# Chunk decays of a state-space layer: from a mask addition on VectorE to products with scaled lower triangles

## The reference

```
acum  = cumsum(dt * A)                       # over the 128 tokens of a chunk
decay[i, j] = exp(acum[i] - acum[j]) for j <= i, else 0
wgt   = (C . B)[i, j] * decay[i, j] * dt[j]
y     = wgt @ x  +  exp(acum) * (C @ h_start)
h_end = exp(acum[last]) * h_start + sum_j exp(acum[last] - acum[j]) dt[j] x[j] B[j]
```

## Time and profile before

| | |
|---|---|
| time before, median of 3 runs | 2368.07 us (2365.31 to 2373.49) |
| profiled execution, its time | 2380.31 us |
| its span | 2378.5 us |
| busy: TensorE products, weight loads | 1704.0 us (72%), 1171.4 us (49%) |
| busy: VectorE, ScalarE, GpSimd | 1596.6 us (67%), 492.7 us (21%), 930.1 us (39%) |
| granted TensorE clock, mean of the span | 0.817 of 2.4 GHz |

### The profile page before, as it was taken

One profiled execution on the slowest core, in us unless ns is written; L12 is line 12 of the kernel. 1 busy time (PEld: TensorE's weight loads), 2 busy tenths in 40 slices (PEclk: granted clock), 3 DMA queues, 4 the chain that ended last, 5 costly groups with the idle time before them and its releaser, 6 DMA issues.

```text
span 2378.5 us, 30817 instructions
## 1 busy us (share of the span) xinstructions
PE 1704.0 (72%) x10511; PEld 1171.4 (49%) x10511; DVE 1596.6 (67%) x4212; ACT 492.7 (21%) x1458; POOL 930.1 (39%) x840
## 2 busy tenths in 40 slices
PE   7999976687897898966999979993544444344434
PEld 7899966443686776754678757670100000000000
DVE  5634178877668537988566775637288878877854
ACT  3335233200144123222123320110011000010000
POOL 0000001145433443533554554657644444444441
PEclk9999988757899999988999989997655655555656
DMA  6487757279999999966999999989999999999995
GB/s 233 140 270 253 245 186 235 80 265 375 393 387 359 385 404 333 365 227 203 344 397 335 388 348 395 393 343 341 394 422 421 421 421 421 418 422 414 409 421 226
DMA packets 179628, 798.80 MB, mean 336 GB/s; under 512 B 20720, under 2 KB 20976, under 8 KB 143504
## 3 DMA queue, kind: packets, MB, share of 16 engines
q0 software_dynamic: 119808, 570.48, 61.3%
q1 hardware_dynamic: 57312, 219.39, 25.5%
q10 hardware_dynamic: 2352, 6.95, 1.0%
HBM read 779.88 MB, written 12.14 MB: 333 GB/s over the span
## 4 chain that ended last, share of the span: by engine, by line
PE 17%; DMA 15%; DVE 12%; issue 5%; POOL 4%; ACT 1%; POOLq 0%; DVEq 0%; SPq 0%
PE ps L477 9%; DMA s_exr<-in_uv,s_gidx 5%; DMA s_wr<-in_uv,s_gidx 3%; PE ps L802 3%; DVE s_exr L1697 3%; PE ps L785 2%; DMA s_scr<-in_uv,s_gidx 2%; DMA s_hnr<-in_uv,s_gidx 1%; DMA s_exr<-in_u,s_gidx 1%; DMA s_exr<-in_v,s_gidxT 1%; DMA s_xr<-in_uv,s_gidx 1%; POOL s_exr L1307 1%; POOL s_exr L1352 1%; DMA s_hT<-in_uv,s_gidx 1%; POOL s_exr L1319 1%
## 5 line engine op out<-in xcount | busy, mean ns | idle before, releaser
L477 PE MATMUL ps<-s_hnr,s_wr 128*128 128x256 f32 (+2 forms) x3968 | 672.8, 327 | 54.5 <-ACT s_hist_p L963 36.3
L477 PEld LDWEIGHTS ps<-s_hnr,s_wr 128*128 128x128 f32 x3968 | 603.5, 195 | 133.7 <-issue 89.3
L1307 POOL DMA_INDIRECT s_exr<-in_u,s_gidx x288 | 316.5, 1099 | 901.9 <-DVE s_act_z L1697 492.7
L1697 DVE CUSTOM_DVE_ANT_0 s_exr<-s_exr,s_tbg 128x1024 f32<-128x1024 f32 x407 | 491.7, 1221 | 177.2 <-DMA s_exr<-in_u,s_gidx 116.5
L1319 POOL DMA_INDIRECT s_exr<-in_v,s_gidxT x256 | 280.5, 1096 | 154.5 <-issue 82.6
L802 PE MATMUL ps<-s_exr,s_sw 128*32 128x512 f32 x476 | 157.3, 1044 | 162.9 <-DVE s_sw L1726 162.9
L785 PE MATMUL ps<-s_exr,s_zb 128*32 128x512 f32 x1072 | 156.4, 668 | 60.0 <-DMA s_exr<-in_v,s_gidxT 51.4
L1352 POOL DMA_INDIRECT s_exr<-in_uv,s_gidx x119 | 138.1, 1161 | 149.1 <-PE ps L802 120.9
L802 PEld LDWEIGHTS ps<-s_exr,s_sw 128*32 128x32 f32 x476 | 25.0, 156 | 244.8 <-DVE s_sw L1726 192.8
L802 PE MATMUL ps<-s_scr,s_sw 128*32 128x512 f32 x160 | 88.6, 1037 | 60.4 <-DVE s_sw L1726 51.0
L802 PE MATMUL ps<-s_wr,s_sw 128*32 128x512 f32 x152 | 86.0, 1050 | 62.0 <-DVE s_sw L1726 62.0
(11 more groups left out here) (313 smaller groups left out, 2684.3 us busy)
## 6 DMA issues: line engine op xcount, KB each, us to landing
s_wr<-in_wstream SPq DMA_DIRECT2D x360, 512.0 KB
s_tbg<-s_h2e ACTq DMA_DIRECT2D x36, 128.0 KB
s_exr<-in_u,s_gidx POOLq DMA_INDIRECT x288
s_exr<-in_v,s_gidxT POOLq DMA_INDIRECT x268
s_xr<-in_sample_h_in SPq DMA_DIRECT2D x4, 1024.0 KB, 8.1
s_scr<-in_sample_h_in SPq DMA_DIRECT2D x4, 1024.0 KB, 7.8
out_sample_h_out<-s_xr SPq DMA_DIRECT2D x4, 1024.0 KB, 8.5
out_sample_h_out<-s_scr SPq DMA_DIRECT2D x4, 1024.0 KB
```

The source lines that it names most:

```text
L477: last = pe.matmul(ps[:, o % 2, 0:n], wring[:, slot, k, :], rhs[:, k, :], start=k == 0, stop=k == KT - 1)
L1307: pool.indirect_dma_start(uring[n % URING], None, a["u"], bass.IndirectOffsetOnAxis(ap=gidx[:, i % 2, s:s + 1], axis=0)).then_inc(u_in[n % ...
L1697: dve.tensor_tensor_reduce(out=u, in0=u, in1=tbg[:, i % 2, :], scale=1.0, scalar=0.0, op0=ALU.mult, op1=ALU.add, accum_out=act_z[:, i % 2, ...
```

## The change

The decays' argument is made whole by TensorE: with `low` the strictly lower triangle, `seg` = `low` scaled by the column DA[:, head], and seg^T @ tri = sum of DA over j < s <= i, which is acum[i] - acum[j] for j <= i and 0 above. ScalarE scales the triangle (four Copies with a scale column, `scaled_low`) and reads the product from PSUM with one Exp of 128x512. The mask now sits on `cbs`: VectorE evicts the C-B products times `tri`. `segments` and its semaphore go; the bank is free when the Exp is done (`dec_ready`), and `seg` when the products are done (`ab_mm`).

```diff
-_CONSTS = [("ident", P), ("tri", P), ("mneg", P), ("ones", P), ...
+_CONSTS = [("ident", P), ("tri", P), ("low", P), ("ones", P), ...
 # TensorE, ssd_chunk
                 def acum_rows(hb):
+                    pe.wait_ge(low_ready, c * 8 + hb + 1)
                     if not (first and hb == 0):
-                        pe.wait_ge(seg_ready, c * 8 + hb)
+                        pe.wait_ge(dec_ready, c * 8 + hb)
                     for k in range(4):
-                        h = 4 * hb + k
-                        last = pe.matmul(ps[:, 0, k * CH:(k + 1) * CH], dac[:, h:h + 1].to_broadcast([P, P]), tri,
+                        last = pe.matmul(ps[:, 0, k * CH:(k + 1) * CH], seg[:, k * CH:(k + 1) * CH], tri,
                                          start=True, stop=True)
                     last.then_inc(ab_mm, 1)
 # TensorE, samples and the end of a piece: seg_ready becomes dec_ready
 # ScalarE, ssd_chunk
+                def scaled_low(hb):
+                    if not (first and hb == 0):
+                        act.wait_ge(ab_mm, c * 8 + hb)
+                    for k in range(4):
+                        last = act.activation(seg[:, k * CH:(k + 1) * CH], cc("low"), ACT.Copy,
+                                              scale=DA[:, c, 4 * hb + k:4 * hb + k + 1])
+                    last.then_inc(low_ready, 1)
                 def decays(hb):
-                    act.wait_ge(seg_ready, c * 8 + (hb + 1))
+                    act.wait_ge(ab_mm, c * 8 + (hb + 1))
                     if not (first and hb < 2):
                         act.wait_ge(wgt_ready, c * 8 + (hb - 1))
-                    for k in range(4):
-                        last = act.activation(dec[:, hb % 2, k * CH:(k + 1) * CH], seg[:, k * CH:(k + 1) * CH],
-                                              ACT.Exp, bias=nac[:, 4 * hb + k:4 * hb + k + 1])
-                    last.then_inc(dec_ready, 1)
+                    act.activation(dec[:, hb % 2, :], ps[:, 0, :], ACT.Exp).then_inc(dec_ready, 1)
+                act.wait_ge(dt_ready, pc.p + 1)
+                scaled_low(0)
                 act.wait_ge(small_sb, c + 1)
                 act.wait_ge(h_done, c * NG)
                 act.activation(cdec[:], ps[:, 4, NH:2 * NH], ACT.Exp)
                 act.activation(ed[:], el[:], ACT.Exp).then_inc(ed_ready, 1)
-                act.wait_ge(cb_mm, c + 1)
-                act.wait_ge(wgt_ready, c * 8)
-                act.activation(cbs, ps[:, 1, :].rearrange("p (g t) -> p g t", t=CH), ACT.Copy).then_inc(cb_sb, 1)
                 decays(0)
+                scaled_low(1)
...
                 for g in range(NG):
                     decays(2 * g + 1)
+                    if g + 1 < NG:
+                        scaled_low(2 * g + 2)
...
                     if g + 1 < NG:
                         decays(2 * g + 2)
+                        scaled_low(2 * g + 3)
 # VectorE, ssd_chunk
-                segments(0)
+                dve.wait_ge(cb_mm, c + 1)
+                dve.tensor_tensor(cbs, ps[:, 1, :].rearrange("p (g t) -> p g t", t=CH), bc1(tri, NG), ALU.mult).then_inc(cb_sb, 1)
                 scaled_x(0)
                 scaled_x(1)
-                segments(1)
...
                     weights(2 * g)
-                    if g + 1 < NG:
-                        segments(2 * g + 2)
                     weights(2 * g + 1)
-                    if g + 1 < NG:
-                        segments(2 * g + 3)
```

More of the change, by code:

```diff
@@ L58 @@
     NPAR += _w
-_CONSTS = [("ident", P), ("tri", P), ("mneg", P), ("ones", P), ("tri_s", DEC), ("mneg_s", DEC), ("blk_s", DEC),
+_CONSTS = [("ident", P), ("tri", P), ("low", P), ("ones", P), ("tri_s", DEC), ("mneg_s", DEC), ("blk_s", DEC),
            ("bcol", DEC_B), ("sel", DEC), ("iota", TOPK)]
@@ L335, in hybrid_layer @@
             sems("small_mm small_sb cb_mm cb_sb tr_mm tr_free_x tr_free_b")
-        ed_ready, xs2_ready, ab_mm, seg_ready, dec_ready, wgt_ready = \
-            sems("ed_ready xs2_ready ab_mm seg_ready dec_ready wgt_ready")
+        ed_ready, xs2_ready, ab_mm, low_ready, dec_ready, wgt_ready = \
+            sems("ed_ready xs2_ready ab_mm low_ready dec_ready wgt_ready")
         intra_mm, pair_mm, eas_ready, inter_mm, inter_read, intra_read, y_done, s_mm, h_done = \
@@ L661, in samples @@
                 pe.wait_ge(eas_ready, c1 * NG)
-                pe.wait_ge(seg_ready, c1 * 8)
+                pe.wait_ge(dec_ready, c1 * 8)
                 pe.wait_ge(h_done, c1 * NG)
@@ L865, in _ @@
                     pe.wait_ge(sm_h, NG * DEC_B)
-                pe.wait_ge(seg_ready, 8 * pc.c_end)
+                pe.wait_ge(dec_ready, 8 * pc.c_end)
                 pe.wait_ge(h_done, NG * pc.c_end)
@@ L1447, in ssd_chunk @@
                 first = c == 0
[L1449 to L1454, removed]
                 def weights(hb):
@@ L1910, in _constants @@
     put("tri", i[:, None] <= i[None, :])
-    put("mneg", np.where(i[:, None] <= i[None, :], 0.0, NEG))
+    put("low", i[:, None] > i[None, :])
     put("ones", np.ones((P, P)))
```

## The result

The changed kernel takes 2397.31 us (median of 4 runs, 2394.59 to 2399.87), the kernel before 2368.6 (4 runs, 2365.31 to 2373.49): ratio 1.0121, 95% interval 1.0106 to 1.0137, so 28.7 us more. The forecast was 16.5 us more. By time that is nearer to rival (a), the clock, at 2400, than to the forecast's 2384.5. The sign, the places and the waits were right; something in these places costs nearly twice as much.

A forecast was written before the change was run, and what follows sets the result against it. Chunk 0 was taken as nearly full on TensorE, later chunks as set by an order of waits. Terms 7.1 + 6.4 + 3.0 = 16.5 us on the median 2368.07 gave 2384.5 us, range 2373 to 2402.

The forecast's parts named there:

- rival (a): All chunks: TensorE's clock falls in the new gaps; 31.5 us more, time 2400; chance 0.18.
- The wait: Chunk 0's groups: odd decay product waits for the copies, starting at 5.36 instead of 3.37; 3 x 1.99 = 6.0 us.
- the upper bound: ScalarE, each half-group: four scaled Copies take 1.28 us, as four Exps with a bias column do; lower bound 0.60.
- one multiply of 0.69 in place of the copies: Twelve group stalls: a VectorE multiply would take 0.59 out of each, 7 us of 16.5, and still leave a loss.
- The start of chunk 0: Chunk 0's start: later copies delay the third decay product from 82.19 to 83.3; 1.1 us.
- The nine groups: Chunks 1 to 3: copies delay the state decay, 0.55 in three full-clock groups, 0.8 in six half-clock ones; 6.4 us.
- The starts of chunks 1 to 3: Scaling of x starts later: 0.2 and 0.4 us in chunks 1 and 2, 2.4 in chunk 3; together 3.0.
- chunk 0 is at 0.96 and 1.9 us is below both: Argument against the clock falling: chunk 0's 1.9 us gaps are shorter than idle stretches of 2.61 and 5.41 us.
- if the gaps cost clock in chunk 0: Chunk 0: one of three stated signs that the forecast would be wrong; no size of its own.
- (b): Chunks 1 to 3: slots, gathers or ready rings hide the delay, leaving chunk 0's 7.1 us; time 2375; chance 0.17.
- (c): Nine groups of chunks 1 to 3: VectorE is the bound, up to 11 us saved; time 2357; chance 0.08.
- VectorE's saved work has no share: Chunk 3: the chain that ended last doesn't go through the removed mask addition, which is missing among the largest lines.

The follow-up runs named there:

- the first experiment: Changed kernel with ScalarE's copies one step earlier and, in chunk 0, the Exp ahead of the gate's Tanh: 2397.72 us, ratio to before 1.0015.
- The third experiment: Changed kernel with the scaled triangles made by one VectorE multiply per half-group in place of ScalarE's four Copies: 2401.34 us, ratio to before 1.0031.
- The second experiment: Changed kernel with six idle products in the copies' wait of each of chunk 0's three groups: 2416.32 us, ratio to before 1.0066.
- the two filled kernels: Idle products on TensorE, twelve per group in chunks 1 to 3: changed kernel (chunk 0's gaps also filled) 2374.76 us; kernel before 2363.89 us.
- The last two experiments: Changed kernel with copies earlier in groups and at chunk starts: 2367.76 us; the same plus twelve idle products per group in chunks 1 to 3: 2362.79 us.
- the last experiment: Changed kernel with copies earlier in groups and at chunk starts, plus twelve idle products per group in chunks 1 to 3: 2362.79 us, ratio to before 0.9975.
- the three filled kernels: Twelve idle products per group in chunks 1 to 3: changed kernel (chunk 0 also filled) 2374.76 us, kernel before 2363.89, changed kernel with earlier copies 2362.79.
- the first four experiments: Changed kernel with copies earlier, chunk 0's gaps filled, triangles on VectorE, or one Copy in half-groups 3, 5, 7: ratios to before 1.0015, 1.0066, 1.0031, 1.0008.
- the last four: Idle products in the changed kernel, in the kernel before; changed kernel with copies earlier at starts too, without and with idle products: ratios 1.0041, 0.999, 1.0012, 0.9975.

## Why the prediction was right in its places and too low in its size

**The wait (chunk 0, 6.0 us).** Shown. Gap 1.91, 1.91 and 1.97 us for 1.92; the waits view puts it on the copies; the first experiment takes it away by order alone. The four copies took 1.26 to 1.28, the upper bound that the forecast chose. What it did not say is that only 1.1 of each gap are the copies' and 0.85 the place of the Exp that empties the bank; this is where the sentence "one multiply of 0.69 in place of the copies would take 0.59 out of each of 12 stalls", 7 us, falls short. The third experiment saved 15.6: the sentence leaves the multiply in the copies' place behind the Exp, the experiment makes it ahead, which takes 1.06 out of each gap of chunk 0, and part of the 15.6 is the clock behind shorter gaps.

The Trainium skill, "ScalarE: Activation LUTs", section "What ACT_TABLE_LOAD costs", gives an ACTIVATE of N elements whose bias is a pointer operand about 280 + 0.833 N ns, an estimate of 387 for N = 128. The changed kernel's trace has a median of 390 for its 128 Copies with a scale column, which agrees.

**The start of chunk 0 (1.1 us).** The step happened, but its size can't be read in the two traces: the even product of the first group comes 9.80 us behind the small sums, 10.07 before. In the changed kernel's trace the C-B products and the first decay product ran at the full clock (1.14 and 1.06), in the one of before at the half (1.80 and 1.91), 1.5 us less. Of the ten kernels four had this start at the full clock (all with the change) and six at the half (four of these with it); whether the change has a part in that stays open. With 1.5 us added back, the start lost 1.2. The second experiment has the same start with the first decay product at the half clock (1.91), as before: its even product comes 10.83 us behind the small sums, 0.8 later than before, with C-B products 0.36 us shorter, so again about 1.1. Its chunk 0, which has this start and no slow gate unit, costs 52.57 - 45.72 = 6.9 us for the 7.1 forecast.

**The nine groups (6.4 us).** Here the forecast failed: they cost 16.5 us. Its positions were right (product at T+2.59, warm group T+6.30 at 1153.54 for T+6.35). Its clock was not: it took three groups as warm and six as they were. After the change one of nine ran as the warm one. In the two filled kernels an undisturbed group takes 6.31 against 5.81, 0.50 for the 0.55 forecast, and the nine together 59.6 against 54.45, 5.15 more. The changed kernel's chunks 1 to 3 in the second experiment repeat the reading: nine groups 72.3 us, one of them warm.

**The starts of chunks 1 to 3 (3.0 us).** What chunks 1 to 3 lost beyond their groups is 19.8 - 16.5 = 3.2 us. In chunk 3 the scaling of all x starts 11.86 us behind the small sums (1108.37 to 1120.23) against 9.85 (1088.79 to 1098.64): 2.0 later, at the low end of the 1.9 to 2.9 forecast. It is not a fixed cost: the first weights multiply, 18.75 us behind the small sums before and 20.77 after, came at 21.2 to 22.6 in the four other kernels that keep this start. The last two experiments, which make the triangles ahead of the softmax, have it at 19.24 and 19.25.

**The clock: the step that failed.** The sum has no term for it. The forecast priced it as rival (a), 31.5 us with a chance of 0.18, and argued against it: "chunk 0 is at 0.96 and 1.9 us is below both", that is below the 2.61 and 5.41 us of idleness whose ends it had read in the trace. Both readings were of one idle stretch ahead of one product, and no row showed a gap as short as 1.9 us. They do not carry over: in chunk 0 such a gap sent TensorE to 1.2 GHz in two of three groups, and in chunk 2 it was 1.19 us more behind a wait of 2.62 that did. The size: the change costs 16.0 us in the chunks with the clock held (the forecast's 16.5) and 28.8 without; the 12.8 between them, 3.4 in chunk 0 and 9.5 in the others, are the clock's by this account, for the 15 of rival (a). The starts of chunks 1 to 3 differ by 5.1 us between the filled kernels and by 3.2 between the unfilled, which this account takes from the clock; by the groups alone it has 14.6, 3.2 in chunk 0 and 11.4 in the nine. That the 16.0 meets the 16.5 is in part luck: chunk 0 and the groups cost less than forecast (5.7 and 5.15 for 7.1 and 6.4), the starts more. Rival (a) as well had its parts differently, 6 for chunk 0 and 9 for the rest. One of the forecast's own signs of being wrong, "if the gaps cost clock in chunk 0", came true; its range held 2397 because it reached up to take in this rival. That the filling products act by the clock is shown by the durations, 1.95 for 3.50 and 3.25 of the same product, with the copies just as late.

The Trainium skill, "TensorE: Matmul & The Clock Gate", section "What's actually happening" of Part 1, has the throttled clock as the default that activity releases. The filled kernels agree: idle products brought the same gate unit from 3.50 and 3.25 to 1.95 us.

**The other rivals.** (b), hidden in chunks 1 to 3: false, their 19.8 us are in the time. (c), VectorE the bound: false as it stood, since the copies were never ready by T+1.3; the last experiment meets its condition. Once they are ready and the clock is held, in the last experiment, a group takes 5.20 instead of 5.80, half of the 1.2 us that (c) gave. So the reading that VectorE's saved work has no share was not right for a warm group; unfilled, the clock hides it.

**What stays open.** Why the clock still fell in one group of nine in each of the three filled kernels, and how short a gap is safe: with gaps of 0.37 to 0.43, 0.85 to 0.91 and 1.04 to 1.10 us every gate unit of chunk 0 ran at the full clock, behind the two gaps of 1.91 us neither did, and behind the one of 1.97 it did, so length alone doesn't decide. And whether the time follows the chunks one for one, as the forecast assumed. Against the kernel before, the chunks of the first four experiments are 7.0, 23.6, 13.2 and 7.6 us longer and their ratios give 3.6, 15.8, 7.4 and 1.9 us; those of the last four, in the order above, are 9.9 and -6.1, 2.7 and -9.6, and the ratios give 9.7 and -2.4, 2.8 and -5.9. All but the -6.1 lie within the interval of their ratio, but the time moves by less in nearly all.

## What to carry to other kernels

A bank or a buffer that gets a new producer brings that producer's whole queue with it: before the durations are summed, write down what stands ahead of the new instruction in its engine's list, and see whether it could be issued one step earlier; here the order decided over 21 of 28.8 us, the clock behind the gaps included. Where TensorE runs near full and a change opens gaps of a microsecond or two in its list, price the work behind each gap at half the clock as well, and take that case as likely as the other. To tell waiting from a slower clock, put idle products in the gap: what then goes away without the wait moving is the clock's. Put no more of them than the wait holds: where TensorE came late, twelve idle products held up the real ones by 2 us.

## What the runs showed of the hardware that I had not expected

- Behind two of three gaps of 1.9 us, in a stretch that had run at a granted clock of 0.96, the next sixteen product records took 3.50 and 3.25 us instead of 1.95. With 1.60 us of idle products in the gap, and 0.37 us left of it, all took 1.95.
- Work that computes nothing shortened the chunks of a tuned kernel: twelve products in each group of chunks 1 to 3 took 6.1 us from the chunks of the kernel before (its time is not told apart), 12.3 from the version with the earlier copies (218.08 to 205.80; ratio 1.0012 to 0.9975), and 19 from the changed kernel together with the filled gaps.
- Moving one set of copies forward in a queue, and in chunk 0 the next Exp, was worth 21.9 us of chunk time (244.24 to 222.39), more than the whole forecast.
